# A decoder step on one core: the first tile ahead of the first weights, three stages in one block, the causal mask on VectorE

## What is computed

```python
xn = rmsnorm(x); p = xn @ w_in      # columns: q latent 384 | kv latent 256 | rotary key 32 | gates A, B | r k v, LoRAs
# A: latent attention, 8 heads: q = c_q @ w_uq; k, v = c_kv @ w_ukv, per-head RMS norms, rotary parts
#    prompt: s = where(kpos <= qpos, q.k * SCALE, NEG); softmax(s) @ v
#    sample: the same over 32 cached pages of 128 positions per sequence (running max, sum and value), then the 4 new ones
# B: RWKV-7, 8 heads: S = S*w - (S kk)(kk a)^T + v k^T per token; y = S r; group norm, bonus, gate
mixed = concat(o_a * silu(gate_a), o_b)
x1 = x + mixed @ w_out
y  = x1 + (p_l @ w_ple) * sigmoid(rmsnorm(x1) @ w_ple_gate)
```

## Time and profile before

| | |
|---|---|
| median of 3 runs | 1372.71 us (1370.44 to 1373.48) |
| profiled execution | 1373.91 us, its span 1372.0 us |
| TensorE busy | 1301.0 us, 95%; idle 71 us |
| VectorE, ScalarE, GpSimd busy | 707.8, 459.9, 150.8 us |
| mean granted clock of TensorE | 0.973 of full speed |

### The profile page before, as it was taken

The page is one execution under the profiler, slowest core; times in us unless marked ns, Lnnn a source line. Parts: engine busy times, 40 slices in busy tenths (PEclk is TensorE's granted clock), DMA queues, the critical chain, the costliest instruction groups (busy, mean ns, idle before and its releaser), DMA issues. The chain is left out here.

```text
span 1372.0 us, 26075 instructions
## 1 busy us (share of the span) xinstructions
PE 1301.0 (95%) x9543; PEld 750.1 (55%) x9543; DVE 707.8 (52%) x1749; ACT 459.9 (34%) x1108; POOL 150.8 (11%) x182
## 2 busy tenths in 40 slices
PE   5999999699999999999989999999999999989898
PEld 3545677556666666555445445666544444445343
DVE  3001436644665656555737876667666666520321
ACT  3001343233343433332434433434344444310220
POOL 0000314400020201114402230000000000000000
PEclk9999999789999999999999999999999999998999
DMA  5422121101111111131141113221334221101000
GB/s 206 155 74 54 32 62 32 52 19 37 37 37 37 37 37 37 37 71 36 40 129 41 40 39 113 97 90 43 86 112 116 68 69 53 49 0 35 16 16 35
DMA packets 82995, 81.49 MB, mean 59 GB/s; under 512 B 18946, under 2 KB 76611, under 8 KB 82868
## 3 DMA queue, kind: packets, MB, share of 16 engines
q1 hardware_dynamic: 80452, 73.87, 18.1%
q10 hardware_dynamic: 2416, 5.96, 1.2%
HBM read 75.72 MB, written 4.07 MB: 58 GB/s over the span
## 5 line engine op out<-in xcount | busy, mean ns | idle before, releaser
L500 PE MATMUL PS<-wk,c_T 128*128 128x512 f32 x1024 | 500.8, 612 | 0.0
L627 DVE TENSOR_REDUCE ssq<-sq__69 128x8 f32<-128x512 f32 x256 | 175.4, 685 | 221.1 <-ACT sq__69 L554 218.7
L500 PEld LDWEIGHTS PS<-wk,c_T 128*128 128x128 f32 x1024 | 176.3, 192 | 163.0 <-issue 145.7
L554 ACT ACTIVATE sq__69<-PS 128x512 f32<-128x512 f32 x256 | 152.8, 597 | 320.5 <-PE PS L500 320.2
L455 PE MATMUL PS<-cst,c_ring 128*128 128x128 f32 x512 | 83.0, 287 | 24.7 <-DVE c_ring L663 10.1
L1470 PE MATMUL PS<-xnT,w_ring 128*128 128x276 f32 x416 | 104.7, 409 | 0.0
L455 PEld LDWEIGHTS PS<-cst,c_ring 128*128 128x128 f32 x512 | 60.4, 147 | 69.7 <-issue 45.0
L1304 PE MATMUL PS<-w_ring,xnT 128*128 128x424 f32 x256 | 95.3, 530 | 2.1 <-DMA w_ring<-in_w_in 2.1
L1470 PEld LDWEIGHTS PS<-xnT,w_ring 128*128 128x128 f32 x416 | 79.9, 195 | 21.9 <-issue 4.1
L1304 PEld LDWEIGHTS PS<-w_ring,xnT 128*128 128x128 f32 x256 | 48.5, 193 | 46.8 <-issue 44.3
L2655 PE MATMUL PS<-w_g,nT 128*128 128x512 f32 x128 | 56.0, 594 | 0.0
(11 more groups left out here) (534 smaller groups left out, 1873.3 us busy)
## 6 DMA issues: line engine op xcount, KB each, us to landing
c_ring<-in_cache_ckv SPq DMA_DIRECT2D x256, 128.0 KB, 2.8
w_ring<-in_w_in SPq DMA_DIRECT2D x4, 1696.0 KB, 14.4
w_ring<-in_w_in SPq DMA_DIRECT2D x9, 512.0 KB, 5.0
r_ring<-in_cache_kpe SPq DMA_DIRECT2D x256, 16.0 KB, 1.8
w_o<-in_w_out SPq DMA_DIRECT2D x8, 512.0 KB, 3.7
w_g<-in_w_ple_gate SPq DMA_DIRECT2D x8, 512.0 KB, 3.6
xn<-in_x_prompt SPq DMA_DIRECT2D x4, 512.0 KB, 7.0
w_ring<-in_w_in SPq DMA_DIRECT2D x2, 1024.0 KB, 5.8
```

Source lines behind the costliest of these rows:

```text
L500: mm = pe.matmul(PS[:, NORM[v % 2], :], c_T[:, u % 2, k, t * P:(t + 1) * P], wk[:, k], start=(k == 0), stop=(k == 1))
L554: nc.scalar.activation(sq_[:, v % 2, :], PS[:, NORM[v % 2], :], ACT.Square).then_inc(no_sb, 1)
L627: dve.tensor_reduce(ssq[:, u % 2, t * H:(t + 1) * H], sq_[:, v % 2, :].rearrange("p (h c) -> p h c", h=H), AX.X, ALU.add).then_inc(red_sb, 1)
```

## The change

1. **Start.** SyncE issues tile 0, then chunk 0 of the weights, then the other tiles, sample and states, then chunk 1. `turn(i + 1)` is done inside `project(i)`, behind its fourth of eight products. ScalarE and VectorE copy tile 0 out before they go on to the norm of tile 1, and the constants' DMA is issued a little later.
2. **Ring.** The first two `turn_c` take a slot each. VectorE makes the first copy (`turned_c(0)`) ahead of the memset, which is in the second slot; `values(0)` waits for it instead of the first transpose.
3. **Preparation.** Most steps of the loops over p move to the front of the next projection or one projection forward; `sums` and `bonuses` stand earlier, the last `bonuses` inside projection 12. `kept(3)` of VectorE and `scaled(3)` of GpSimd now come before the copies of projection 12, and VectorE makes the first ring copy right behind these, ahead of `shift(11)`.
4. **One block.** Chunks, sequences and latents become functions (`chunk_pe`, `seqs_pe`, `lat_pe`, ...) that one block calls in turn; two `recycle()` and two block ends are gone. Semaphores stand for them: `rows_kept` (GpSimd has copied the sample's rows), `wkv_sb` and `half_sb` in front of the sequences, `so_sb` in front of the latents. One more slot stands at the top of the sequences (`SEQ_SLOTS` 24, one fewer in the tail). SyncE loads the sample states as soon as the last chunk has made its products with `BT`, and stores the prompt's state one slot later; its wait for all stores behind the sequences stays.
5. **Mask.** `scores(u)` is one product; VectorE adds the mask in PSUM ahead of the maximum.

The diff, without what is only indented anew and with the moves of 3 cut to VectorE's and TensorE's:

```diff
             def values(u):
+                if u == 0:
+                    pe.wait_ge(ring_ready, 1)
...
-            pe.wait_ge(ring_ready, 1)
             turn_c(0, 0)
+            yield
             turn_c(0, 1)
+            yield
...
+            turned_c(0)
+            yield
             dve.memset(c_ring[:, :, :, KVL:KVL + 1], 1.0).then_inc(ring_ready, 1)
-            turned_c(0)
+            yield
...
+                tile_in(0)
                 weights(0)
+                for i in range(1, NT - 1):
+                    tile_in(i)
+                sp.dma_start(xn[0:NS, NT - 1, :], io["x_sample"]).then_inc(x_in[NT - 1], 16)
+                sp.dma_start(stx[:], io["state_shift"]).then_inc(x_in[NT], 16)
                 weights(1)
...
                 for p in range(RWC):        # VectorE
+                    if p == 7:
+                        new_max()
+                        key_norms(0)
+                        ends(0)
...
+                    if p == 11:
+                        key_norms(3)
+                        kept(2)
+                        ends(3)
+                    if p == 12:
+                        kept(3)
                     dve.wait_ge(rw_ps, p + 1)
...
+                    if p == 12:
+                        on_dve.go(1)
                     if p >= 1:
                         shift(p - 1)
...
+                        if c == 0 and k == KD // 2 - 1:
+                            turn(i + 1)
...
-                turn(1)
-                project(0)
-                turn(2)
...
+                for u in range(NM):
+                    project(u)
                 turn(5)
...
-                        if part == 0 and p in (7, 8):
-                            sums(p - 7)
-                        if part == 0 and p in (10, 11):
-                            sums(p - 8)
-                        if part == 0 and p == 12:
-                            bonuses(2)
+                        if part == 0 and p == 7:
+                            new_scores()
+                            sums(0)
+                        if part == 0 and p == 8:
+                            new_weights()
+                            sums(1)
+                        if part == 0 and p in (11, 12):
+                            bonuses(p - 9)
...
+                    if p in (9, 10):
+                        sums(p - 7)
+                        bonuses(p - 9)
                 pe.wait_ge(cur_act, RWC)
                 pe.wait_ge(cur_dve, RWC)
                 on_pe.go(2)
-                bonuses(PAIRS - 1)
-                on_pe.go(PREP_SLOTS - 2)
+                on_pe.go(PREP_SLOTS)
...
+        def seqs_sp(sp):
+            sp.wait_ge(l_ps, NP)
+            sp.wait_ge(rows_kept, 1)
             sp.dma_start(s0_nat[:].rearrange("v b (h k) -> v b h k", h=H),
                          io["state_wkv"].rearrange("b h v k -> v b h k")).then_inc(st_in, 16)
-                on_sp.go(SEQ_SLOTS - 4)
+            on_sp.go(1)
+            sp.wait_ge(wkv_sb, 1)
+            store(sp, io["wkv_prompt"].rearrange("h v k -> v h k"), wkv_t[:].rearrange("v j x k -> v (j x) k"))
+            on_sp.go(SEQ_SLOTS - 5)
...
+        def seqs_pe(pe):
+            on_pe.go(1)
+            pe.wait_ge(rows_kept, 1)
+            pe.wait_ge(wkv_sb, 1)
+            pe.wait_ge(half_sb, NP)
...
             pe.wait_ge(w_lat2, 32)
+            pe.wait_ge(so_sb, BS)
...
+        with nc.Block() as block:
+            @block.sync
+            def _(sp):
+                chunk_sp(sp)
+                seqs_sp(sp)
+                lat_sp(sp)
...
-                    pe.matmul(bank(u % 2)[:, 0:w], qT[:, h, i * P:(i + 1) * P], k_T[:, h, 0:w], start=True, stop=False)
-                    pe.matmul(bank(u % 2)[:, w - P:w], ident, con("causal"), start=False, stop=True).then_inc(sc_ps, 1)
+                    pe.matmul(bank(u % 2)[:, 0:w], qT[:, h, i * P:(i + 1) * P], k_T[:, h, 0:w], start=True, stop=True
+                              ).then_inc(sc_ps, 1)
...
                     dve.wait_ge(sc_ps, u + 1)
+                    V(dve.tensor_tensor(bank(u % 2)[:, w - P:w], bank(u % 2)[:, w - P:w], con("causal"), ALU.add))
```

More of the change, by code:

```diff
@@ L1524, in build @@
         AR_s = place("AR_s", [P, 2, PAIRS, NS])
+        wkv_t = place("wkv_t", [HN, PAIRS, 2, HN])
         gt = ua[:].rearrange("p (c j) k -> p c j k", c=2)
@@ new lines, in chunk_pe @@
+                mm.then_inc(l_ps, 1)
+                for h in range(H):
+                    for ck in HALVES:
+                        mm = pe.matmul(eight(2, ck)[:, at_head(h), :], gram[ck, at_head(h), 2, :],
+                                       vn[ck, i, h * HN:(h + 1) * HN], start=True, stop=True)
+                mm.then_inc(w_ps, 1)
+                on_pe.go(2)
+                pe.wait_ge(low_sb, 3 * i + 1)
+                products(0, gram[:, :, 0], low[:, 0])
+                products(1, low[:, 0], gram[:, :, 0]).then_inc(y2_ps, 1)
@@ new lines, in chunk_pe @@
+                on_pe.go(1)
+                pe.wait_ge(u5_sb, i + 1)
+                pe.wait_ge(low_sb, 3 * i + 3)
+                turns(3, ua)
+                products(0, low[:, 2], ua).then_inc(t5_ps, 1)
+                on_pe.go(1)
+                pe.wait_ge(t5_sb, i + 1)
+                products(1, pa[:, 0], pa[:, 1]).then_inc(u6_ps, 1)
+                on_pe.go(1)
+                pe.wait_ge(u6_sb, i + 1)
+                for o in range(H):
+                    for ck in HALVES:
+                        mm = pe.matmul(bank(2 + o // 4)[ck, (o % 4) * P:(o % 4 + 1) * P], ub[ck, o, :], aw[ck, o, :, :],
+                                       start=True, stop=True)
```

1511 lines of the change are left out of this document (739 added, 772 removed).

## The result

The changed kernel took 1354.2 us (median of four, 1351.9 to 1355.4) where the kernel before took 1372.1 beside it: ratio 0.987, 95% interval 0.985 to 0.989. The gain is 18 us where 28 were forecast; the time lies 1.2 us above the range's upper end. The program was run again beside the experiments, with 1350.0 (1348.7 to 1355.0) and 1350.4 us (1347.4 to 1353.3), at ratios of 0.983 [0.981, 0.986] and 0.984 [0.983, 0.986]. All fourteen executions lie between 1347.4 and 1355.4 us, mean 1351.5; the mean of 67 executions of the kernel before is 1373.9. So the gain is better put at 22 us: of the ten microseconds that are missing, four are the chance of the first measurement (its chip and executions), and six are not.

What follows compares the result with a forecast made beforehand. TensorE, busy 1301 of 1372 us, was taken as the bound, gaining from removed work or its 71 us idle. Terms 1.5 + 1.0 + 9.5 + 6.2 + 3.5 + 6.5 = 28.2 us gave a median of 1344.5 us, range 1335 to 1353.

Steps and rivals of the forecast that it cites:

- The start: Kernel start: weights issued ahead of most tiles let projection 0 begin at 14.75 instead of 17.93 us; gain 1.5 us.
- The projections: Projections of the RWKV columns: two waits go (2.0 us), the last bonuses move before the end (loss 1.0); gain 1.0 us.
- The end of the projections: Behind the last projection (end X): VectorE's copy comes earlier, SyncE's page issues then set the block's end; gain 9.5 us.
- Chunks to sequences: Barrier between chunks and sequences: its 4.57 us idle and 1.65 us of half clock go; gain 6.2 us.
- Sequences to latents: Barrier before the latents: a 3.8 us wait for weights replaces 5.8 us; gain 3.5 us, bounds 0 and 7.9.
- The shifted slots: Latents: one slot later, waits for VectorE may be two more or fewer; 2 us either way, left to the range.
- The mask: Attention, 32 units: mask products worth 7.0 us leave TensorE, VectorE's adds bring 0.5 us of waits; gain 6.5 us.
- rival (a): Second barrier: SyncE's stores and page issues hold the latent weights as long as it did; 1349.5 us, chance 0.16.
- (b): Attention: VectorE becomes the bound, mask gains 2 us, the shift costs 3 in latents and attention; 1352 us, chance 0.14.
- (c): SyncE doesn't hold the first block, less half clock, shorter latents' wait: 7.4 us more gain; 1337 us, chance 0.15.
- (d): Attention: the add holds every unit, deciding from 2.0 us per add; slower, 1375 us or more, chance 0.02.
- (e): Waits replacing the barriers stop engines as long, VectorE's copy still comes last behind the projections; 1361 us, chance 0.05.

Runs made afterwards that it cites:

- e11: The changed kernel with SyncE's issues in the old order, all tiles and states before the first weights: 1353.5 us, ratio 0.985 to the kernel before.
- e8: The changed kernel with SyncE's page issues of steps 2 and 3 moved behind the barrier after the preparation: 1348.1 us, ratio 0.980.
- e6: The changed kernel with a block end and barrier put back between sequences and latents: 1351.7 us, ratio 0.984.
- l1: The changed kernel with a fourth slot of page work at the top of the latents, one fewer in the tail: 1348.8 us, ratio 0.982.
- e2: The changed kernel without the extra slot at the top of the sequences, the tail taking it instead: 1353.4 us, ratio 0.984.
- e1: The changed kernel with the mask as a TensorE product again, VectorE adding nothing: 1354.9 us, ratio 0.987.
- The third profile: Profile from another run of the changed kernel, unaltered, beside later experiments: median 1350.4 us, profiled span 1345.3 us.

## Why the prediction was right in direction and wrong in size

The forecast was 1344.5 us and the first measurement 1354.2. In its profile (1353.0 against 1343.8 us of span) the difference of 9.2 us is 4.6 in the sequences, 4.2 in the latents, 2.6 in the units and 1.1 elsewhere behind X, less 3.3 up to the chunks. The step that failed is the price of the shifted ring: the forecast put it at nothing in the sum and "2 us either way" in the range, and the latents came out 3.6 to 4.2 us above it in all three profiles, nearly all of it waits in two of them. Beside it the mask's term was too large by some 2 us and that of the second boundary by some 2 to 3; the sequences' 4.6 us are half clock that other executions of the same program don't have, and for which the range had no room. Term by term:

- **The start (1.5 us).** Right. The projection starts at 14.78 us (forecast 14.75) and the wait in it is gone: the tile's transposes begin behind its first half at 20.57. The old order costs 1.3 us in e11; in the forecast's own account the order was to bring the start from 17.93 to 14.75, and e11 shows 16.25 to 14.78 of it. The worst case that the forecast took from the Trainium skill (page "DMA: Bandwidth & Descriptors", section "Queues, rings and completion order": completion is not first in, first out) did not come: the weights, issued second, were there by 14.78 us.
- **The projections (1.0).** Both waits went as argued, save 0.3 us. X came 5 us sooner where 2.5 were forecast; the profile of before had 5.1 us of half clock that two other profiles with the same preparation show as 1.7 (X at 255.6 and 256.9 us). Against those the gain is 0.8 to 2.9 us. So the 2.5 of both terms is about right, and the other 2.7 us of the first comparison are for the most part luck: the profile of before had 3.4 us more half clock here than the two others.
- **The end of the projections (9.5).** Right in size and in mechanism: 10.1 us, the restart at X + 22.1 (forecast 22.2), SyncE's last issue at X + 20.5, and e8 moves the restart by moving the issues.
- **Chunks to sequences (6.2).** Right by the stages (292.5 to 293.5 us against 292.5 forecast), and the transposes of `vT_s` run at full clock behind the slot. The barrier put back costs 5.1 us, but only 1.65 of it at the barrier.
- **Sequences to latents (3.5).** The forecast of this boundary was precise (a wait for the weights of 3.8 us: 3.9, 3.3; for the next page 0.7: 1.1) and yet the term is 0.4 to 1.8 us, since the barrier put back costs only that. What was mis-sized is the clock: 0.8 us for half clock behind the wait, where TensorE ran for 5.6 us at 0.50 (687 to 693 us), 2.8 us of busy time lost, about as much as behind the barrier in e6 (2.6). That is rival (a) in effect: the weights are waited for, and ahead of their issue SyncE waits 1.8 us for the stores. The upper bound of this term, 7.9, comes to 8.1 by its own numbers (704.47 - 695.7 - 0.7); nothing hangs on it.
- **The shifted slots (2 us either way).** This is the step that was most under-sized. The latents became 5.1 to 5.7 us longer instead of 1.5. Of this 2.8 to 4.2 us are waits: `c_T` 3.9 us where there were none, `dots_s` 0.6 instead of 3.4, up to 1.2 more for `acc`, 1.1 for the page, 0.7 more at the barrier in front of the attention. The rest, 0.7 to 2.9, is half clock. With the ring one quarter turn further on they are 128.2 us (l1), one turned back 129.7 (e2). It could not be costed from one profile, which shows one position; four of them were needed.
- **The mask (6.5).** Mis-sized twice. The products were priced by the distance of two starts, 0.22 us each, and are worth 0.17 (5.3 instead of 7.0 us); and the adds, 0.300 us as forecast, bring 0.8 us of waits instead of 0.5. Putting it back (e1) costs about 4 us, 4.5 in the units by the profiles. In the first profile 1.5 us of half clock came on top.
- **The half clock.** The forecast took it for something that follows a gap. It also falls without one, in the sequences, with 5 us of difference between executions of one program; why it does isn't known. The range, taken from the terms alone, should have been some 3 us wider on either side for it.
- **The rivals.** (b) gave the best time (1352) for a reason that isn't so: VectorE doesn't bound the attention, but its share of the shift (3 us) is near what happened. (c), (d) and (e) fell.

The third profile, the one with the least half clock, is only 1.5 us above the forecast's own sum (1345.3 against 1343.8), but not because the terms held: 3.6 in the latents, 1.2 in the units and 1.1 in the tail are made up for by 4.4 up to the latents, 3.0 of it in front of X, which is the luck named above. The mean of the fourteen executions, 7 us above the forecast, adds the half clock that the others had more of, and the 1.2 us by which the forecast had been set lower to stand for the median.

## What to carry to other kernels

A step that moves one stream against another has a price of its own, as large as a barrier's, and one profile doesn't show it: try the positions, since they are cheap to run. A wait that is exchanged for a barrier should stand in front of the first instruction that needs it and not at the stage's head; two slots of cover were worth 5.3 us here by the medians and 8.5 by the ratios. Before a term is read off two profiles, profile the same program twice, and take the granted clock out of the difference.

## What was unexpected in the hardware

- The granted clock of a busy TensorE fell to 0.50 in the sequences without idle time: 3 us into a run of products of 4 and 32 columns (604.8 to 612.0 us), and stayed there for the wide products behind it until 618. A fall at this place stands in all nineteen profiles. One program lost 17.7, 22.7 or 26.8 us to half clock, and its spans stand in the same order (1345.3, 1347.0, 1353.0 us). The Trainium skill, page "TensorE: Matmul & The Clock Gate", section "Why this matters for your kernels", advises against gaps between bursts; here the fall in the gap-free narrow products (5 us, 607.9 to 618) cost more than the one behind the longest wait inside a block (2.8 us, 687 to 693).
- An add that writes PSUM from VectorE costs nearly what the product to SBUF does: 0.300 us for a 128x128 add from and to PSUM, 0.277 us for the product from PSUM to SBUF.
- A block whose TensorE had ended 5.7 us before was held by SyncE's 20 DMA issues and what it does between them, 256.7 to 274.8 us; with 8 of them it restarted 3.9 us sooner (e8).
